# The order of four queues in the recurrence of a three-block network: masks, first factors and attention's items moved

## The reference

```
def step(state, inp):                       # RWKV-7, one token
    r_t, w_t, k_t, v_t, kk_t, b_t = inp
    sa = einsum('bhvk,bhk->bhv', state, -kk_t)
    state = state * w_t + sa (x) b_t + v_t (x) k_t
    return state, einsum('bhvk,bhk->bhv', state, r_t)

scores = einsum('bnqhgd,bnkhd->bnhgqk', qb, kb) * HEAD_DIM ** -0.5   # blocks of 128, previous and own
scores = where(band, scores, -inf)
probs = softmax(concat([scores, sink]))[..., :-1]
out = einsum('bnhgqk,bnkhd->bnqhgd', probs, vb)
```

## Time and profile before

| | us |
|---|---|
| median of 3 runs | 2889.28 (2884.97 to 2896.59) |
| profiled execution | 2887.84 |
| its span | 2886.1 |
| PE busy | 2754.6 (95%) |
| DVE busy | 1424.6 (49%) |
| POOL busy | 1153.8 (40%) |
| ACT busy | 1004.7 (35%) |
| mean granted TensorE clock | 0.979 |

### The profile page before, as it was taken

The page is one execution under the profiler, slowest core; times in us unless marked ns, Lnnn a source line. Parts: engine busy times, 40 slices in busy tenths (PEclk is TensorE's granted clock), DMA queues, the critical chain, the costliest instruction groups (busy, mean ns, idle before and its releaser), DMA issues. The chain is left out here.

```text
span 2886.1 us, 39162 instructions
## 1 busy us (share of the span) xinstructions
PE 2754.6 (95%) x16698; PEld 2249.6 (78%) x16698; DVE 1424.6 (49%) x1771; ACT 1004.7 (35%) x1388; POOL 1153.8 (40%) x503
## 2 busy tenths in 40 slices
PE   7899999887999999998999999998999999999997
PEld 6778887676888888777888888886887778888785
DVE  4974337675467345763625343105477555233422
ACT  4232234133333322446323333222325543222541
POOL 3434443531444444473444444444234323322342
PEclk9999999988999999999999999999999999999998
DMA  5445322100333323222222333334556222222232
GB/s 193 144 142 151 101 93 80 45 4 22 117 114 128 104 99 93 83 88 73 88 95 95 95 95 99 99 95 151 197 143 184 76 68 88 81 66 66 73 95 73
DMA packets 115213, 288.37 MB, mean 100 GB/s; under 512 B 34832, under 2 KB 46032, under 8 KB 114384
## 3 DMA queue, kind: packets, MB, share of 16 engines
q1 hardware_dynamic: 115040, 285.87, 31.4%
HBM read 261.94 MB, written 26.25 MB: 100 GB/s over the span
## 5 line engine op out<-in xcount | busy, mean ns | idle before, releaser
L428 POOL TENSOR_TENSOR weight_ring_r<-weight_ring,weight_hi_r 128x1024 fp32r<-128x1024 f32 (+2 forms) x412 | 1041.0, 2527 | 1607.4 <-ACT weight_hi_r L421 1607.4
L421 ACT ACTIVATE weight_hi_r<-weight_ring 128x1024 fp32r<-128x1024 f32 (+2 forms) x412 | 447.7, 1088 | 1492.4 <-PE acc L631 1118.8
L625 PE MATMUL acc<-p_r,weight_hi_r 128*128 128x512 f32 x1776 | 701.1, 395 | 31.8 <-ACT weight_hi_r L421 19.4
L626 PE MATMUL acc<-scr_r,weight_hi_r 128*128 128x512 f32 x1120 | 440.1, 393 | 0.0
L631 PE MATMUL acc<-p_r,weight_ring_r 128*128 128x512 f32 x1776 | 436.9, 389 | 0.0
L625 PEld LDWEIGHTS acc<-p_r,weight_hi_r 128*128 128x128 f32 x1776 | 336.6, 190 | 106.2 <-ACT weight_hi_r L421 20.7
L626 PE MATMUL acc<-p_r,weight_hi_r 128*128 128x512 f32 x1008 | 392.2, 389 | 0.0
L631 PEld LDWEIGHTS acc<-p_r,weight_ring_r 128*128 128x128 f32 x1776 | 333.9, 188 | 69.5
L626 PEld LDWEIGHTS acc<-scr_r,weight_hi_r 128*128 128x128 f32 x1120 | 212.9, 190 | 46.3 <-issue 2.9
L880 DVE SCALAR_TENSOR_TENSOR x<-acc,x 128x512 f32<-128x512 f32 x56 | 36.9, 688 | 382.6 <-PE acc L631 382.5
L625 PE MATMUL acc<-scr_r,weight_hi_r 128*128 128x512 f32 x544 | 219.9, 404 | 2.2 <-ACT weight_hi_r L421 2.2
(11 more groups left out here) (548 smaller groups left out, 3816.5 us busy)
## 6 DMA issues: line engine op xcount, KB each, us to landing
weight_ring<-in_weights SPq DMA_DIRECT2D x372, 512.0 KB, 3.5
weight_ring<-in_weights SPq DMA_DIRECT2D x32, 704.0 KB, 4.0
weight_ring<-in_weights SPq DMA_DIRECT2D x8, 640.0 KB, 3.8
s_inner<-p SPq DMA_DIRECT2D x16, 256.0 KB, 4.4
s_outer<-p SPq DMA_DIRECT2D x16, 256.0 KB, 4.7
s_inputs<-p SPq DMA_DIRECT2D x16, 256.0 KB, 2.6
p<-s_inputs SPq DMA_DIRECT2D x8, 512.0 KB, 5.4
p<-s_inner SPq DMA_DIRECT2D x8, 512.0 KB, 7.4
```

What stands on the lines that cost most here:

```text
L421: self.nc.scalar.activation(self.r.weight_hi[:, ahead, 0:width], self.weight_ring[:, r, 0:width], ACT.Copy)\
L428: self.nc.gpsimd.tensor_tensor(rest, raw, hi, ALU.subtract).then_inc(self.weights_split, 1)
L625: pe.matmul(product.out(b, m), hi, op.hi(kx), start=kx == 0, stop=False)
L626: pe.matmul(product.out(b, m), hi, op.lo(kx), start=False, stop=False)
```

## The change

Nothing is added or taken out; instructions change their places in the queues.

- GpSimd: the scaling of unit n - 2 stands behind the masks of level n (before: unit n - 1), scaling 3 behind the levels, then the four additions of `ln_b` (line 2161), then the scalings of units 4 to 7. Before, all scalings stood ahead of the additions.
- VectorE: both starts of Tm come before the starts of T. Mask and max of unit 0 move from level 0 to level 1, mask 1 stands in the middle of level 1.
- TensorE: keys move from ahead of level 0's first zm to behind its first zt, values behind the second; scores 0 move into level 1 behind its Y, scores 1 behind its first zt.
- Units: scores at k = 1, 5, 9 (units 5, 6, 7), outs at 2, 6, 10 (units 2, 3, 4), turns at 3, 7, 11 (units 3, 4, 5), with masks, maxima, exponentials and copies to match. Before: scores at 1, 7, outs at 3, 9, turns at 5, 11, and scores 7 in the chunk loop.
- Chunk loop: outs of units 5, 6, 7 at c = 0, 2, 4 and turns of 6 and 7 at c = 1, 3. Before: scores 7 at c = 0 and an out or a turn in each later chunk, to c = 7.

```diff
@@ tensor, levels
-                if n == 0:
-                    pe.wait_ge(q["tt_start"], 2)
-                    att.pe_keys(pe)
-                else:
-                    att.pe_scores(pe, n)
+                if n:
+                    att.pe_scores(pe, 0 if n == 1 else n)
...
                     if n == 0 and d == 0:
+                        pe.wait_ge(q["tt_start"], 2)
+                        att.pe_keys(pe)
+                    elif n == 0:
                         att.pe_values(pe)
-                    elif n == 0:
-                        att.pe_scores(pe, 0)
+                    elif n == 1 and d == 0:
+                        att.pe_scores(pe, 1)
@@ tensor, units
-                if k in (1, 7):
-                    att.pe_scores(pe, 5 + k // 6)
-                if k in (3, 9):
-                    att.pe_out(pe, 2 + k // 6)
-                if k in (5, 11):
-                    att.pe_turn(pe, 3 + k // 6)
+                if k in (1, 5, 9):
+                    att.pe_scores(pe, 5 + k // 4)
+                if k in (2, 6, 10):
+                    att.pe_out(pe, 2 + k // 4)
+                if k in (3, 7, 11):
+                    att.pe_turn(pe, 3 + k // 4)
@@ tensor, chunks
-                if c == 0:
-                    att.pe_scores(pe, 7)
-                elif c % 2:
-                    att.pe_out(pe, 4 + c // 2)
-                else:
-                    att.pe_turn(pe, 4 + c // 2)
+                if c in (0, 2, 4):
+                    att.pe_out(pe, 5 + c // 2)
+                if c in (1, 3):
+                    att.pe_turn(pe, 6 + c // 2)
@@ scalar
+                if k == 0:
+                    att.act_exp(act, 4)
+                if k in (2, 6, 10):
+                    att.act_out(act, 2 + k // 4)
+                if k in (3, 7, 11):
+                    att.act_turned(act, 3 + k // 4)
+                if k in (3, 8):
+                    att.act_exp(act, 5 + k // 8)
+            att.act_exp(act, 7)
@@ gpsimd
                 if n == 0:
                     att.pool_queries(pool)
-                else:
-                    att.pool_scale(pool, n - 1)
-            for u in range(N - 1, UNITS):
-                att.pool_scale(pool, u)
+                elif n >= 2:
+                    att.pool_scale(pool, n - 2)
+            att.pool_scale(pool, 3)
             for i in range(PAIRS):
                 nc.gpsimd.tensor_scalar(p[:, RW_BON + i, :], p[:, RW_BON + i, :], core.vcol("ln_b", i), None, ALU.add).then_inc(q["raised"], 1)
+            for u in range(4, UNITS):
+                att.pool_scale(pool, u)
@@ vector, setup and levels
                 v.tensor_tensor(duo(RW_TM, d), duo(RW_TM, d), rep(eye), ALU.add).then_inc(q["tm_start"], 1)
+            for d in range(2):
                 dve.wait_ge(q["a_read"], d + 1)
...
-                    att.dve_mask(dve, n)
+                    att.dve_mask(dve, 0 if n == 1 else n)
                 for d in range(2):
+                    if n == 1 and d:
+                        att.dve_mask(dve, 1)
...
+                        if n == 1 and d == 0:
+                            att.dve_max(dve, 0)
...
-                if n == 0:
-                    att.dve_mask(dve, 0)
-                att.dve_max(dve, n)
+                if n:
+                    att.dve_max(dve, n)
@@ vector, units and chunks
-                if k in (1, 7):
-                    att.dve_mask(dve, 5 + k // 6)
-                if k in (5, 9):
-                    att.dve_sum(dve, 4 + k // 9)
-                    att.dve_max(dve, 5 + k // 9)
+                if k in (1, 5, 9):
+                    att.dve_mask(dve, 5 + k // 4)
+                if k in (3, 7):
+                    att.dve_sum(dve, 4 + k // 4)
+                if k in (3, 7, 9):
+                    att.dve_max(dve, 5 + k // 4)
...
-                if c == 1:
-                    att.dve_sum(dve, 6)
-                    att.dve_max(dve, 7)
-                if c == 3:
-                    att.dve_sum(dve, 7)
+                if c < 2:
+                    att.dve_sum(dve, 6 + c)
```

More of the change, by code:

```diff
@@ L2134, in _ @@
                 a(of_chunk(RW_TM, c), from_banks(4), ACT.Square).then_inc(q["o_read"], 1)
-                if c == 1:
[L2136 to L2140, removed]
+                if c in (0, 2, 4):
+                    att.act_out(act, 5 + c // 2)
+                if c in (1, 3):
+                    att.act_turned(act, 6 + c // 2)
             act.wait_ge(q["var"], 1)
@@ L2213, in _ @@
                     squares(c - 1)
-                if c == 1:
-                    att.dve_mask(dve, 7)
                 dve.wait_ge(q["w"], c + 1)
```

## The result

The changed kernel takes 2877.18 us, the median of 10 runs (2871.03 to 2886.67), beside 2891.26 us for the kernel before (10 runs, 2884.97 to 2897.56): a ratio of 0.9952, 95% interval 0.9938 to 0.9966, which leaves out 1. The forecast was a saving of 13.0 us and 2876.3 us; measured are 14.1 us. The size came out, but in part by luck: setup gained much less than forecast, and a charge for the clock in levels and units was not needed.

What follows compares the result with a forecast made beforehand. TensorE was taken as the bound, idle at level ends for GpSimd's masks, with half clock behind. Terms 5.0 + 14.0 - 6.1 + 3.4 + 0.7 = 17.0, less charges 3.5 and 0.5, save 13.0: 2876.3 us, range 2867 to 2884.

Steps and rivals of the forecast that it cites:

- The levels: Levels 1 to 4: masks no longer behind a scaling, so 44.75 us where 58.73 stood, 14.0 less.
- The idle time of 3.05 at zt: Level 2: masks hold VectorE's small operations, so Tm is late and TensorE idles from 17.05 to 20.1.
- Rival D: Levels: VectorE's blocked max takes the mask's place in full, 14.0 shrinks to about 5; 2885 us, chance 0.07.
- Setup: Setup: both Tm first, keys and values later, so level 1 starts at 571.5 instead of 576.47, 5.0 us less.
- The charge for the clock: Levels and units: half clock behind gaps of 3.05, 2.85 and 2.4 us, charged at 3.5 us.
- B: Half clock in most gaps, and setup's third mask ahead of the second T: saving 6.5, 2882.8 us, chance 0.14.
- C: Units: the clock falls in the first gap and stays at half, costing 21.8 us more; 2894 us, chance 0.04.
- Units: Twelve units: three more attention items and three new waits make 28.1 us where 22.0 stood, 6.1 more.
- Three waits for a mask: Units: outs 2, 3, 4 wait for VectorE's masks of scores, idle 2.85, 2.4 and 1.2 us.
- Chunk loop: Chunk loop: attention items fall from 8 to 5 and chunk 1 loses a max; together 3.4 us less.
- Tail: End of the chunk loop: last out's copy three chunks earlier, so ScalarE's table load no longer delays the root; 0.7 less.
- Rival A: Levels and units: nothing holds VectorE, levels 2 and 3 take 10.0, units 25.7; some 2869 us, chance 0.15.

Runs made afterwards that it cites:

- e1: Changed kernel with GpSimd's scaling of unit n-1 again ahead of the masks of level n+1; 2890.66 us, ratio 0.9998 to the kernel before.
- e12: Kernel before with one edit: GpSimd's scaling of unit n - 2 instead of n - 1 behind the masks of level n; 2878.68 us, ratio 0.9957.
- e10: Changed kernel with three wide filler matmuls in setup and attention's outs one product later in the units; 2871.62 us, ratio 0.9930 to the kernel before.
- e2: Changed kernel with VectorE's old order in setup, the first T again ahead of the second Tm; 2882.87 us, one run.
- e3: Changed kernel with GpSimd's four additions of ln_b behind the last scaling; 2876.96 us, one run.
- e4: Changed kernel with attention's items in units and chunk loop, and the additions of ln_b, at their old places; 2877.99 us, ratio 0.9949 to the kernel before.
- e6: Changed kernel with three more 64x64 products as fillers on TensorE in setup, results overwritten; 2868.05 us, one run.
- e7: Changed kernel with attention's outs in the units one product later, two products behind their scores; 2879.30 us, one run.
- e9: Changed kernel with three wide matmuls (128x512) filling TensorE's two idle times in setup; 2875.14 us, ratio 0.9943 to the kernel before.
- e5: Changed kernel with VectorE's small operations of max 1 and 2 behind the next level's mask and first Tm; 2874.85 us, ratio 0.9953 to the kernel before.
- e11: Changed kernel with sixteen more 64x64 products in a row (512 matmuls) in setup behind the second Y, results overwritten; 2901.91 us, one run.

## Why the prediction was right, and where it was not

**The levels** (forecast 14.0 us, measured 12.45). The mechanism was right and is shown from both sides: with the masks' place undone the gain is gone (e1), with that one edit alone it is nearly all there (e12). With the wait for the mask went the half clock behind it. Of the 1.5 us that are missing, level 1 has 0.8 (10.78 for 10.0), of which 0.57 is a gap of issue, and level 4 has 0.6. Level 2 was forecast at 13.1 and is 13.06, but for a mixed reason. VectorE was held as forecast, for 2.03 and 2.28 us. The idle time of 3.05 at zt put down to Tm doesn't show in this execution, since TensorE's gaps of issue (0.51, 0.91, 0.94, 2.36 together) had already made it late by as much. Where these gaps are smaller it does show, at the same zt of level 2. The timeline of TensorE in e10, whose levels are ordered as in the changed kernel (L2190 is VectorE's Tm there):

```profile
591.14 1.03 PE L1971 MATMUL acc<-scr,p 64*64 64x64 f32 x53 [0.39 <-issue]
593.80 2.08 PE L1971 MATMUL acc<-p,scr 64*64 64x64 f32 x64 [1.62 <-DVE p L2190]
```

In e2, e3, e4, e6, e7, e9 and e10 this wait is 0.18 to 1.62 us, and with the gaps of issue in level 2 it makes 1.98 to 2.12 each time. So the held VectorE costs level 2 some 2.0 us of idle time, where 3.05 was forecast, and issue covers all or part of it. e5 shows that the gaps alone give 12.36. Rival D, that VectorE's blocked max takes the mask's place in full, is refuted.

**Setup** (forecast 5.0, measured 2.1; 2.1 to 3.8 over the six executions with this setup). This step failed: it reckoned setup behind the first zm at full clock. The times until the first zm came as forecast: zm at 564.57 where 563.2 and the shift of 1.2 us make 564.4. From there zm took 1.98, zt 3.66 and keys 2.19, where at full clock they take 1.16, 2.04 and 1.98 (e9; keys were put at 1.8). The forecast looked for the clock only behind idle times of 2.9 us or more; here it fell behind 1.00 and 1.62 us of waiting (and 0.67 of issue ahead of them). e9 settles it: with these filled the clock stays at 1.00 and setup is 22.23 (22.15 in e10), near the 21.9 forecast.

**The charge for the clock** (forecast 3.5 in levels and units, measured none there and 2.6 in setup). The windows of levels, units and chunk loop are 1.00: the idle times there came out at 1.48 us or less, not 2.4 to 3.05. The sum was right by luck, because this charge and the setup's miss of 2.9 nearly cancel. Rivals B and C, which live on that clock, are refuted, C's place in the units above all.

**Units** (forecast 6.1 more, measured 5.0). Three waits for the mask came, as forecast, but the first is 0.23 instead of 2.85: its cause, additions of `ln_b` that hold VectorE, isn't there (e3). The prediction had the evidence for it, 0.35 us in the row beside a tensor_scalar of GpSimd, and went by the masks' rows. The SBUF rule weighed there (the Trainium skill, "SBUF — State Buffer", section "Who interferes with whom") is borne out by masks and scalings (2.03, 2.28, 0.85 us) and hardly by the additions, whose instructions read SBUF too (0.29 and 0.16 us; 0.16 and 0.16 without them in e3). The form of GpSimd's instruction alone doesn't decide it: in setup its four queries, tensor_scalar as well, take 0.69 to 2.18 us each, while VectorE's operations with two inputs in SBUF take 1.58 instead of 1.23. Why the additions hold so little stays open. The other two waits came to 1.48 and 0.32 instead of 2.4 and 1.2. Idle time put to issue is 1.18 in the units, less than the 2.03 of before. It grew in the levels, from 0.33 to 3.09, where the forecast had put 0.5 more for the whole stretch and 2.6 came. e7 shows that the waits for the masks could be had back by a later out.

**Chunk loop** (forecast 3.4, measured 4.5). Chunk 1 and the chunks without an item came as reckoned, with 3.69 a chunk where 3.55 was forecast. Not in the forecast were chunk 0, 0.9 shorter, and that chunk 6 became 1.4 shorter and not 1.03 (0.22 of it a gap of issue). Of the 0.9 in chunk 0, 0.60 was a gap of issue in the kernel before; e12 has scores 7 there, no such gap, and 5.12. **Tail** (forecast 0.7, measured 1.26): the table load is over at 684.18, and VectorE waits 0.52 us for the root. In the other kernels with the last out moved the tail is 0.7 to 1.6 shorter than before, and in e4, which has it at its old place, 0.6. So this gain isn't told from scatter.

**Rival A**, nothing holds VectorE (2869), was right for the additions and wrong for masks and scalings. e5, where the small operations are out of the masks' way, shows that it would have paid little in the levels: 45.58 instead of 46.28.

**The whole.** Without charges the forecast was 17.0, by the trace it is 15.3, by the medians 14.1. The terms missed by -2.9 (setup), -1.5 (levels), +1.1 (units), +1.1 (chunk loop) and +0.6 (tail); the charges took 4.0. What the change does besides moving the masks (Tm ahead of T, denser units, later keys) is worth 2.0 us of the stretch, and e12's ratio isn't told from its own.

## What to carry to other kernels

When an engine's late instruction is the wait that ends last, look at what stands ahead of it in its own queue: here one reordered line on GpSimd was nearly the whole gain of a change of five queues. Count the clock behind short idle times of TensorE too, not only behind the long ones, and if there is something harmless to run, fill them with few wide matmuls instead of many small ones (the half clock cost 1.3 to 2.6 us of setup here, too little to be told in the whole time). In a stage of small matmuls, reckon how many instructions a step has before costing its waits: here TensorE stopped once in 128 matmuls and their loads, and level 2, freed of VectorE's hold, became 0.7 us shorter instead of the 2 to 3 that e5 expected. And look at more than one execution before a part of 1 or 2 us is explained: the same setup took 23.14 to 24.81 us.

## What the runs showed of the hardware that was not expected

**TensorE's supply of instructions.** In rows of small products an idle time put to issue comes once in 128 matmul records and their 128 weight loads, at a fixed place of the program. In e11 there is one packet of 16 KB in the instruction queue for each. The stops were 3.45 and 4.00 us apart in e11 and 4.18 and 4.01 in level 2 of the changed kernel (587.47, 591.65, 595.66). Levels 1 to 3 have some 405 records each, 3.16 such steps, which at 3.45 to 4.18 make 10.9 to 13.2 us; measured are 10.78, 13.06 and 12.80 (and 10.15 for level 1 of e5, which has no gap). In the kernel before, and in e1, the levels wait for the masks and the stops hardly show (0.33 and 0.17 us in the levels, 3.09 in the changed kernel). The Trainium skill ("Runtime: NRT & Kernel Launch", section "Instruction fetch mechanics") says that the engine's memory is refilled in blocks of 16 KiB, 256 instructions, and that crossing a boundary is "mostly hidden". The trace agrees on the blocks, and not on the second where 64 records take 1.0 us: there 40% of the time went on it (1.36 of 3.45). Left open is what sets the 3.45 or 4.00. In e11 the packets lie 1 us and more behind the restart and not at its moment, and chunks 5 and 6 pass 144 records in 3.69 us each, 3.3 us per 128, with a packet every 3.4 us and no gap put to issue. That the stops are the supply of instructions is thus argued from their distance and the packets' number; no run changed the supply itself.

**The clock** fell from 1.00 to 0.50 behind waits of 1.00 and 1.62 us in setup, in all six kernels with this setup (0.87 to 1.52 and 1.42 to 1.62 us), and stayed there for different times. In e11 it stayed 1.00 through 28 us in which TensorE was idle for 1.36 to 1.91 us after every 2.10 us of work. So the length of a single idle time doesn't say whether it falls.
